# Sliding-window attention in a two-block layer: keys and values projected together in 512-column products

## The reference

```python
h = _rms_norm(x, norm_mix_g[l])
proj = h @ w_in[l]                      # s_q: 1024 columns, s_k: 256, s_v: 256
q = _rope(_rms_norm(q.reshape(bsz, s, 8, 128), q_g), pos)
k = _rope(_rms_norm(k.reshape(bsz, s, 2, 128), k_g), pos)
v = v.reshape(bsz, s, 2, 128)
# each block of 128 tokens sees its own block and a neighbour on each side
scores = einsum(q, k) * hd ** -0.5      # masked to |distance| <= 128
p = exp(scores - m); o = einsum(p / (p.sum() + exp(sink - m)), v)
```

## Time and profile before

| | |
|---|---|
| median of 3 runs | 2085.43 us (2085.28 to 2085.53) |
| the profiled execution: its own time | 2085.57 us |
| its span in the profile | 2083.8 us |
| TensorE (PE) busy | 2075.8 us, 100% |
| GpSimd (POOL) busy | 1513.9 us, 73% |
| VectorE (DVE) busy | 973.2 us, 47% |
| ScalarE (ACT) busy | 499.4 us, 24% |

### The profile page before, as it was taken

The page is one execution under the profiler, slowest core; times in us unless marked ns, Lnnn a source line. Parts: engine busy times, 40 slices in busy tenths (PEclk is TensorE's granted clock), DMA queues, the critical chain, the costliest instruction groups (busy, mean ns, idle before and its releaser), DMA issues.

```text
span 2083.8 us, 28663 instructions
## 1 busy us (share of the span) xinstructions
PE 2075.8 (100%) x10112; PEld 1732.3 (83%) x10112; DVE 973.2 (47%) x1459; ACT 499.4 (24%) x999; POOL 1513.9 (73%) x1607
## 2 busy tenths in 40 slices
PE   9999999999999999999999999999999999999999
PEld 8888888888788878888888888889888888888887
DVE  6566655521456665755542166436753243222100
ACT  2002111100267674211100054222353122111000
POOL 7888888867864547888877775546645788777675
PEclk9999999999999999999999999999999999999999
DMA  5333333323342223333323332223222333333233
GB/s 158 101 89 102 95 101 91 100 84 95 104 112 83 81 82 86 91 101 91 101 86 94 99 91 81 61 71 102 72 64 70 89 106 97 97 94 101 86 91 96
DMA packets 368163, 192.45 MB, mean 92 GB/s; under 512 B 8672, under 2 KB 364608, under 8 KB 368080
## 3 DMA queue, kind: packets, MB, share of 16 engines
q1 hardware_dynamic: 365280, 186.52, 31.2%
q10 hardware_dynamic: 2800, 4.83, 0.7%
HBM read 189.19 MB, written 2.13 MB: 92 GB/s over the span
## 4 chain that ended last, share of the span: by engine, by line
PE 96%; DVE 2%; ACT 1%; issue 0%; DMA 0%; SPq 0%; DVEq 0%; ACTq 0%
PE PS L575 22%; PE PS L576 22%; PE PS L577 22%; PE PS L889 3%; PE PS L891 3%; PE PS L890 3%; PE PS L905 2%; PE PS L906 2%; PE PS L907 2%; PE PS L734 1%; PE PS L736 1%; PE PS L735 1%; PE PS L697 1%; PE PS L1088 1%; PE PS L677 1%; PE PS L762 1%
## 5 line engine op out<-in xcount | busy, mean ns | idle before, releaser
L558 POOL TENSOR_TENSOR RING<-RAW,RING 128x512 fp32r<-128x512 f32 x704 | 974.9, 1385 | 58.7
L555 POOL TENSOR_SCALAR RING<-RAW 128x512 fp32r<-128x512 f32 x704 | 518.5, 737 | 345.9 <-PE PS L891 89.6
L575 PE MATMUL PS<-XH,RING 128*128 128x512 f32 x1296 | 504.8, 389 | 0.0
L577 PE MATMUL PS<-XH,RING 128*128 128x512 f32 x1296 | 504.2, 389 | 0.0
L576 PE MATMUL PS<-XL,RING 128*128 128x512 f32 x1296 | 504.2, 389 | 0.0
L575 PEld LDWEIGHTS PS<-XH,RING 128*128 128x128 f32 x1296 | 243.3, 188 | 51.4 <-issue 1.1
L577 PEld LDWEIGHTS PS<-XH,RING 128*128 128x128 f32 x1296 | 243.3, 188 | 50.6
L576 PEld LDWEIGHTS PS<-XL,RING 128*128 128x128 f32 x1296 | 243.3, 188 | 50.5 <-issue 0.2
L575 PE MATMUL PS<-HH,RING 128*128 128x512 f32 x528 | 205.6, 389 | 0.0
L577 PE MATMUL PS<-HH,RING 128*128 128x512 f32 x528 | 205.4, 389 | 0.0
L576 PE MATMUL PS<-HL,RING 128*128 128x512 f32 x528 | 205.4, 389 | 0.0
(11 more groups left out here) (342 smaller groups left out, 3411.3 us busy)
## 6 DMA issues: line engine op xcount, KB each, us to landing
RAW<-in_ffn_w_up SPq DMA_DIRECT2D x88, 512.0 KB, 3.7
RAW<-in_w_in SPq DMA_DIRECT2D x52, 512.0 KB, 3.7
RAW<-in_w_ffn_in SPq DMA_DIRECT2D x44, 512.0 KB, 3.7
RAW<-in_ffn_w_down SPq DMA_DIRECT2D x32, 512.0 KB, 3.9
RAW<-in_a_w_in SPq DMA_DIRECT2D x24, 512.0 KB, 3.6
RAW<-in_b_w_qg SPq DMA_DIRECT2D x16, 512.0 KB, 3.7
RAW<-in_w_kvf SPq DMA_DIRECT2D x16, 512.0 KB, 3.9
RAW<-in_w_ffn_out SPq DMA_DIRECT2D x16, 512.0 KB, 3.7
```

Of the source, the lines that this page charges most:

```text
L555: hi = pool.tensor_scalar(WH[s][:, k0_:k1, :], RAW[r][:, k0_:k1, :], 1.0, 1.0, ALU.mult, ALU.mult)
L558: lo = pool.tensor_tensor(WL[s][:, k0_:k1, :], RAW[r][:, k0_:k1, :], WH[s][:, k0_:k1, :].bitcast(F32), ALU.subtract)
L575: pe.matmul(o, WH[s][:, k, :], xh[:, k0 + k, :], start=first and k == 0, stop=False)
L577: mm = pe.matmul(o, WL[s][:, k, :], xh[:, k0 + k, :], start=False, stop=last and k == nk - 1)
```

## The change

Keys and values are made together. The four units of keys and values (now units 4 to 7 of the phase, `KV_UNITS`) no longer hold 128 columns over eight k steps, but 512 columns (256 of keys, 256 of values) over two k steps. `swa_wide(u, t)` makes, for unit u and token block t, 2 k steps x 3 terms = 6 matmuls of 512 columns; the four token blocks accumulate in four whole banks, 6, 7, 2 and 4, over all four units. The other doubles are unchanged, but the order is now queries 0-1, queries 2-3, keys and values, queries 4-5, queries 6-7 (d = 0, 1, 2, 3, 4). Key and value units are thus units 4 to 7, where keys were units 0 and 1 and values units 6 and 7. Turns 0 to 3 and rotates 0 to 3 are those of queries, 4 and 5 those of keys. The scores wait for five rotates (four queries and the key of group 0) where they waited for six. A wide unit is released by itself (`unit_done` + 1 after its four token blocks); a double releases two at once.

```diff
-        X_BANK = (4, 0, 6, 4, 0, 0)
+        X_BANK = (4, 0, None, 0, 0)
+        KV_BANK = (6, 7, 2, 4)
...
+        def normed_chunk(d, c):
+
+            if X_BANK[d] is None:
+                a, b = KV_BANK[2 * c:2 * c + 2]
+                return PS[:, a:b + 1:b - a, 0:2 * P]
+            return PS[:, X_BANK[d] + c, :].rearrange("p (t n) -> p t n", t=2)
...
-        SWA_DOUBLES = (S_K, S_Q, S_Q + 2 * P, S_V, S_Q + 4 * P, S_Q + 6 * P)
-        ph["swa"] = wphase(4, 1, columns(w_in, *[c + u * P for c in SWA_DOUBLES for u in range(2)]), first=2)
+        SWA_FIRST = (0, 2, 4, 8, 10)
+        SWA_LAST = (1, 3, 7, 9, 11)
+        KV_UNITS = range(4, 8)
+        ph["swa"] = wphase(4, 1, columns(w_in, *[S_Q + m * P for m in range(4)]) + [(w_in, 2 * u, KT, lambda i: S_K) for u in range(4)]
+                           + columns(w_in, *[S_Q + m * P for m in range(4, 8)]), first=2)
...
-                        sp.dma_start(RAW[p.raw_slot(j)][:, 0:nk, :], w[:, k0:k0 + nk, bass.ds(c(i), P)]).then_inc(
-                            loaded[p.raw_slot(j)], 16)
+                        to = RAW[p.raw_slot(j)][:, 0:nk, :]
+                        if p is ph["swa"] and j in KV_UNITS:
+                            to = to.rearrange("p (k a) n -> p k (a n)", k=2)
+                            src = w[:, k0:k0 + 2, S_K:S_K + 4 * P]
+                        else:
+                            src = w[:, k0:k0 + nk, bass.ds(c(i), P)]
+                        sp.dma_start(to, src).then_inc(loaded[p.raw_slot(j)], 16)
...
+            def swa_wide(u, t):
+
+                p, j = ph["swa"], KV_UNITS[u]
+                s = p.slot(j)
+                if t == 0:
+                    pe.wait_ge(split_done, p.unit(0, j) + 1)
+                if u == 0:
+                    pe.wait_ge(*[(sem("g_on"), GH * TB), (sem("g_on"), GH * TB), (sem("g_y"), 2 * GH), (sem("sw_x"), 2)][t])
+                o = PS[:, KV_BANK[t], :].rearrange("p (a n) -> p a n", a=4)
+                c = slice(t * P, (t + 1) * P)
+                for r in range(2):
+                    k, cols = 2 * u + r, slice(4 * r, 4 * r + 4)
+                    pe.matmul(o, XH[:, k, c], WH[s][:, cols, :], start=k == 0, stop=False)
+                    pe.matmul(o, XH[:, k, c], WL[s][:, cols, :], start=False, stop=False)
+                    mm = pe.matmul(o, XL[:, k, c], WH[s][:, cols, :], start=False, stop=k == KT - 1)
+                if t == TB - 1:
+                    mm.then_inc(unit_done, 1)
+                elif t == 1 and u == 3:
+                    mm.then_inc(sem("sw_half"), 1)
...
-                pe.wait_ge(sem("sw_rot"), 2 + 4 * (g + 1))
+                pe.wait_ge(sem("sw_rot"), (5, 10)[g])
...
-                for x in range(5):
+                for d in range(2):
                     for t in range(TB):
-                        swa_dense(x, t)
-                        if x in (1, 2, 3) and t == 3:
-                            swa_turn(2 * (x - 1))
-                        if x in (2, 3, 4) and t == 0:
-                            swa_turn(2 * (x - 2) + 1)
+                        swa_dense(d, t)
+                swa_turn(0)
+                for u in range(4):
+                    for t in range(TB):
+                        swa_wide(u, t)
+                        if t == 1 and u in (0, 2):
+                            swa_turn(u + 1)
+                    if u == 1:
+                        swa_turn(2)
+                swa_dense(3, 0)
+                swa_dense(3, 1)
+                swa_turn(4)
+                swa_dense(3, 2)
+                swa_turn(5)
+                swa_dense(3, 3)
                 swa_scores(0, 0)
-                swa_dense(5, 0)
+                swa_dense(4, 0)
                 swa_turn(6)
-                swa_dense(5, 1)
-                swa_dense(5, 2)
+                swa_dense(4, 1)
+                swa_dense(4, 2)
                 swa_turn_probs(0, 0)
                 swa_turn(7)
-                swa_dense(5, 3)
+                swa_dense(4, 3)
 
                 swa_scores(0, 1)
...
                 for n in range(6):
                     swa_square(n)
+                    if n >= 4:
+                        swa_values(n - 4)
                     swa_rsqrt(n)
-                swa_values(0)
-                swa_values(1)
...
-                to, gain = (KR[n], R_SKG) if n < 2 else (QR[n - 2], R_SQG)
+                to, gain = (KR[n - 4], R_SKG) if n in (4, 5) else (QR[n if n < 4 else n - 2], R_SQG)
...
                 swa_norm(1)
                 for x in range(1, 3):
-                    swa_sums(2 * x)
+                    if x == 1:
+                        swa_sums(2 * x)
                     swa_rotate(2 * x - 2)
                     swa_rotate(2 * x - 1)
+                    if x == 2:
+                        swa_sums(2 * x)
                     swa_norm(2 * x)
                     swa_sums(2 * x + 1)
                     swa_norm(2 * x + 1)
-                swa_rotate(4)
-                swa_rotate(5)
                 swa_values_low(0)
                 swa_values_low(1)
+                swa_rotate(4)
                 swa_sums(6)
                 swa_norm(6)
+                swa_rotate(5)
                 swa_sums(7)
                 swa_norm(7)
                 swa_max(0, 0)
```

More of the change, by code:

```diff
@@ L1059, in gla, with swa_dense @@
                         filler(i, n)
-            def swa_dense(x, t):
+            def swa_dense(d, t):
                 free = {0: [(sem("g_st"), 2 * GH * (NCH - 1))] * 2, 1: [(sem("ga_read"), 5), (sem("ga_read"), 4)],
-                        2: [(sem("g_on"), GH * TB)] * 2, 3: [(sem("sw_x"), 1), (sem("sw_x"), 2)],
-                        4: [(sem("sw_x"), 3), (sem("sw_x"), 4)], 5: [(sem("sw_x"), 7), (sem("sw_x"), 8)]}[x]
-                token_block(ph["swa"], 2 * x, t, sem("sw_half"), free, X_BANK[x])
+                        3: [(sem("sw_x"), 3), (sem("sw_x"), 4)], 4: [(sem("sw_x"), 7), (sem("sw_x"), 8)]}[d]
+                token_block(ph["swa"], SWA_FIRST[d], t, sem("sw_half"), free, X_BANK[d])
+            def swa_wide(u, t):
[16 more added lines that the diff above has]
+                    mm.then_inc(sem("sw_half"), 1)
             def swa_turn(n):
@@ L1574, in ga_sigmoid, with swa_chunk_done @@
                 act.activation(SGA[m][:, :], SGA[m][:, :], ACT.Sigmoid).then_inc(sem("ga_sig"), 1)
-            def swa_chunk_done(x, c):
+            def swa_chunk_done(d, c):
                 if c == 0:
-                    act.wait_ge(sem("sw_half"), x + 1)
+                    act.wait_ge(sem("sw_half"), d + 1)
                 else:
-                    act.wait_ge(unit_done, ph["swa"].unit(0, 2 * x + 1) + 1)
+                    act.wait_ge(unit_done, ph["swa"].unit(0, SWA_LAST[d]) + 1)
             def swa_square(n):
-                x, c = divmod(n, 2)
-                swa_chunk_done(x if x < 3 else x + 1, c)
+                d, c = divmod(n, 2)
+                swa_chunk_done(d, c)
                 if n > 0:
                     act.wait_ge(sem("sw_sums"), n)
-                act.activation(SSQ[:, :], PS[:, X_BANK[x if x < 3 else x + 1] + c, :], ACT.Square).then_inc(sem("sw_sq"), 1)
+                act.activation(SSQ[:, :].rearrange("p (t n) -> p t n", t=2), normed_chunk(d, c),
+                               ACT.Square).then_inc(sem("sw_sq"), 1)
             def swa_rsqrt(n):
@@ L1593, in swa_values @@
             def swa_values(c):
-                swa_chunk_done(3, c)
+                swa_chunk_done(2, c)
                 for t in range(2):
-                    cp = act.activation(VSH[c][:, t, :], PS[:, X_BANK[3] + c, t * 2 * P:(t + 1) * 2 * P], ACT.Copy,
+                    cp = act.activation(VSH[c][:, t, :], PS[:, KV_BANK[2 * c + t], 2 * P:S], ACT.Copy,
                                         scale=RT3[:, 2 * c + t:2 * c + t + 1])
@@ L2201, in swa_norm @@
                 dve.tensor_tensor(XN[:, 2 * c:2 * c + 2, :].rearrange("p t (h c) -> p t h c", h=2),
-                                  PS[:, X_BANK[double if double < 3 else double + 1] + c, :].rearrange(
-                                      "p (t h c) -> p t h c", t=2, h=2),
+                                  normed_chunk(double, c).rearrange("p t (h c) -> p t h c", h=2),
                                   SHR.unsqueeze(3).to_broadcast([P, 2, 2, P]), ALU.mult).then_inc(sem("sw_x"), 1)
             def swa_rotate(n):
-                to, gain = (KR[n], R_SKG) if n < 2 else (QR[n - 2], R_SQG)
+                to, gain = (KR[n - 4], R_SKG) if n in (4, 5) else (QR[n if n < 4 else n - 2], R_SQG)
                 if n == 0:
@@ L2254, in swa_values_low @@
                 for t in range(2):
[L2255 removed]
+                    ins = dve.scalar_tensor_tensor(VSL[c][:, t, :], PS[:, KV_BANK[2 * c + t], 2 * P:S],
                                                    RT3[:, 2 * c + t:2 * c + t + 1], VSH[c][:, t, :].bitcast(F32),
```

## The result

| | before | after |
|---|---|---|
| median | 2085.43 us (20 runs, 2084.78 to 2085.95) | 2088.32 us (20 runs, 2087.15 to 2089.55) |
| ratio after / before | | 1.0014, 95% interval 1.0008 to 1.002 |
| span of the profiled execution | 2083.8 us | 2087.0 us |

The change makes the kernel 2.9 us slower, 0.14%: clear of the runs' own spread, within the 0.2% that was named ahead. The runs after the change fall into two groups of ten: 2087.15 to 2087.87 us (median 2087.57) with a mean granted clock of 1.0, and 2088.77 to 2089.55 (median 2089.15) with 0.999. The profiled execution (2088.83 us) is one of the second group.

The account below looks back on a forecast made before the run. TensorE, busy 2075.8 of 2083.8 us at full clock, was taken as the bound. Width -1.24, turn 2 +2.35 and turn 6 +0.9 gave +2.0 us, forecast 2087.4 us, range 2084.2 to 2089.0.

Parts of the forecast that it names:

- The saving by width: TensorE, key and value products: 96 of 512 columns replace 192 of 256, 1.24 us less.
- The rival by which a product's fixed part is only 2.5 ns: Key and value products: a wide product takes 0.238 us, 1.0 us more in all, 2088.4 us; chance 0.05.
- The rival in which the change of bank costs something: Wide products: 16 bank changes at 0.1 to 0.2 us add 1.6 to 3.2 us, 2089.0 to 2090.6; chance 0.06.
- VectorE's norm 3 later by 1.75 us, turn 2 waits: Before turn 2: GpSimd no longer pauses, norm 3 ends at 1448.2 instead of 1446.45; +2.35 us at turn 2.
- its largest risk: Phase of GpSimd's instructions against VectorE's: each small VectorE instruction waits anything from 0 to 1.3 us.
- step 1: Schedule up to turn 0: nothing differs, two doubles and VectorE's first four chunks are done, 1434.10 us.
- step 3: VectorE before turn 2: small instructions wait for GpSimd, norm 3 takes 4.05 us and is done at 1448.2.
- Wait of 0.9 us at turn 6: Turn 6 waits 0.9 us for norm 7, to 1478.1, as rotate 5 now stands between norms 6 and 7.
- The rest moves rigidly: Behind turn 6: rotate 6 and turn 7 have over 1 us to spare, so nothing more is lost.
- The sum, 2087.4 us: Whole kernel: -1.24 from width, +2.35 at turn 2, +0.9 at turn 6, together +2.0 us; this case's chance 0.50.
- the pause stays: Rival: GpSimd's pause stays or small instructions get in between, turn 2 at 1446.5, 2084.9 to 2086.2 us; chance 0.27.
- the clean gain: Rival: VectorE keeps up at turn 6 too, 1.24 to 1.5 us saved, 2084.0 us; chance 0.12.

Follow-up runs that it names:

- turns 2, 3 and 6 later: Changed kernel with turn 2 after block 1 of wide unit 2, turn 3 after block 0 of unit 3, turn 6 behind the last double's block 1: 2084.34 us.
- the pause put back: Changed kernel with one more wait: GpSimd splits unit 8 only when wide unit 1 has been used, so it pauses as before the change: 2086.01 us.
- putting it into the kernel before: Kernel before the change with two extra GpSimd subtractions, inputs in SBUF, behind unit 7 in GpSimd's pause: 2086.55 us.
- turn 2 one block later: Changed kernel with turn 2 moved behind token block 0 of wide unit 2, turn 3 left where it was: 2087.25 us.
- the first four edits: Changed kernel with GpSimd's pause restored (2086.01 us), turns 2 and 3 moved later (2085.24), turn 6 moved later (2086.73), or all three turns moved later (2084.34).
- turn 6 later: Changed kernel with turn 6 moved behind token block 1 of the last double: 2086.73 us.

## Why the prediction was right, and what it lacked

1. **The saving by width, 1.24 us.** Right in mechanism, a little too large. With the waits taken away the section is 1.29 us shorter and the kernel 1.1, but 0.24 of the 1.29 is the old delay at turn 2: the width is worth 1.05 us. One reason shows in the chain: behind turn 1 the first twelve wide products of the kernel with turns 2, 3 and 6 later take 0.232 us each and the rest 0.227, where the forecast had 0.226 for all. The rival by which a product's fixed part is only 2.5 ns is out: it left 0.24 us for the width. (Its own product time is slightly off: 2 x 0.1195 us less 2.5 ns is 0.2365, not 0.238 us; the 1.0 us that follows fits 0.2365.) The rule that it took from the Trainium skill ("TensorE: Matmul & The Clock Gate", Back-to-back issue gap) is given there for a single matmul by itself and not for a stream. The rival in which the change of bank costs something is out too: in the kernel with turns 2, 3 and 6 later no step of 0.14 us more shows at any of the 16 changes.
2. **VectorE's norm 3 later by 1.75 us, turn 2 waits.** Right in mechanism, place and size. Forecast done at 1448.2, measured 1447.80 + 0.34 = 1448.14; sum to norm 4.05 forecast, 4.03 measured; wait 2.35 forecast, 2.26 measured. Shown by taking the cause away (the pause put back, 2086.01) and by putting it into the kernel before (2086.55). How GpSimd's and VectorE's instructions would meet, which the prediction called its largest risk, came out as reckoned, and not by the luck of one execution: with turn 2 one block later the same stretch took 4.01 us. (Its step 1 has four chunks done by turn 0; only norms 0 and 1 are, and its step 3 counts rightly from there.)
3. **Wait of 0.9 us at turn 6.** Right in place and size: the waits view has 3.0 - 2.3 = 0.7 us for it, and the turn itself took 0.66 in place of 0.44, together 0.9; moving the turn gained 1.0. The wait is as long, 0.7 us, where the one at turn 2 is short or gone, so it doesn't come from norm 3. That it comes from rotate 5 standing between norms 6 and 7 was not tested: no run has another order on VectorE there.
4. **The rest moves rigidly.** Right as far as the runs tell: the kernels with the waits removed or shortened by one of the first four edits land within 0.2 us of what was expected; with turn 2 one block later, where turn 3 then waits 1.1 us, the miss is 1.05. The first scores were forecast 1.1 us later than before; they start 2.8 us later in the profiled execution, 1.2 without the 1.6 of the low clock.
5. **The sum, 2087.4 us.** The ten runs at full clock have 2087.57. What was left out is a term, not a step: behind a wait of 2.3 us, TensorE came back at 1.2 GHz in half of the executions, which cost 2089.15 - 2087.57 = 1.6 us in each and raised the median to 2088.32, so the forecast median is 0.9 us too low. The trace has the same: 6 x 0.20 + 0.11 us of products and 0.3 us of transposes, 1.6 us. Of the rivals "the pause stays" and "the clean gain" neither happened.

What stays open is why a wait of this length costs the clock in one execution and not in the next. Counted by the mean granted clock, and with the wait as each kernel's one profiled execution has it, it came in none of the 99 runs of the nine kernels whose waits in this section are at most 1.1 us, in 12 of 31 with one of 2.2 to 2.3 us (10 of 20 of the changed kernel, 2 of 11 with turn 6 later), and in 8 of 11 with one of 3.2 us. That the low clock goes with the long waits is clear; between 2.2 and 3.2 us the runs are too few to say more.

## What to carry to other kernels

An optimisation of the busiest engine shortens the cover of the engines that it waits for, the work that it has while they finish theirs: look for the step where the helper is on time by less than what is gained (here 0.06 us), and move that step along with the gain. Finer-grained release of buffers isn't free either: it lets a producer fill a pause in which another engine had a shared resource to itself. And a wait of a few microseconds on TensorE is to be priced with the clock that may come after it, not by its length alone.

## What the runs showed of the hardware that was not expected

- In the profiled execution of the changed kernel a stand-still of TensorE of 2.26 us, behind a stretch at full clock, was followed by one at 1.2 GHz (granted clock 0.51 from 1448 to 1451 us). By their mean granted clock, 12 of 31 runs of the two kernels with this wait had such a stretch; it cost 1.6 us.
- VectorE instructions of 128x4 elements with inputs in SBUF took 0.15 to 0.17 us beside GpSimd memsets and up to 1.25 us beside GpSimd instructions that read SBUF. The Trainium skill ("SBUF — State Buffer", Who interferes with whom) states this difference between reading and only writing, and the runs agree.
